# Gate units of the state space part given out row by row, convolution taps between a rope and two norms, and four smaller moves in a two-block transformer kernel

## The reference, cut to what matters

```
first_block:   xn = rmsnorm(concat(16 meta tokens, x));  proj = xn @ w_in -> q, k, v, r, a_low, u, z_gla, z_ssm
   o     = rmsnorm(gla_chunked(q, k, v, log_a)) * silu(r)      # 4 heads, key 128, value 256, chunks of 64 tokens
   y_gla = o @ w_o_gla
   y_s   = s5_ssm(u, ...)                                      # 64 groups of 16 channels, 64 complex states each
   glu   = gelu(y_s) @ w_glu + b_glu;  y_ssm = glu[:, :1024] * sigmoid(glu[:, 1024:])
   mixed = sigmoid(z_gla) * y_gla + sigmoid(z_ssm) * y_ssm
   h = h + rmsnorm(mixed @ w_out)
   h = h + rmsnorm(square(relu(rmsnorm(h) @ w_ff1)) @ w_ff2)
second_block:  z = modulated_norm(x) @ w_in_2 -> q_lat (384), kv_lat (256), k_rope (32), conv_in (1024), gates (2048)
   q, k, v from rmsnorm(q_lat) @ w_uq and rmsnorm(kv_lat) @ w_ukv, rope on 32 of 96 channels; 8 heads of attention
   u = glu_a * sigmoid(glu_b);  u = causal_depthwise_conv(u, 31 taps, 512 channels);  y_conv = silu(layernorm(u)) @ w_conv_out
   y = (g_attn * (attn @ w_o_attn) + g_conv * y_conv) @ w_out;  x = x + gate * y
   x = x + gate * hierarchical_moe(norm(x))                    # 4 groups of 8 experts, two chosen of one group
   return rmsnorm(x)
```

## Time and profile before

| what | us |
|---|---|
| median of 3 runs (lowest, highest) | 1719.71 (1713.06, 1719.83) |
| the profiled execution: its time | 1717.65 |
| the profiled execution: its span | 1715.8 |
| PE busy (matmuls) | 1647.7 |
| DVE busy | 1187.0 |
| ACT busy | 738.9 |
| POOL busy | 321.9 |

### The profile page before, as it was taken

One profiled execution on the slowest core, in us unless ns is written; L12 is line 12 of the kernel. 1 busy time (PEld: TensorE's weight loads), 2 busy tenths in 40 slices (PEclk: granted clock), 3 DMA queues, 4 the chain that ended last, 5 costly groups with the idle time before them and its releaser, 6 DMA issues.

```text
span 1715.8 us, 20745 instructions
## 1 busy us (share of the span) xinstructions
PE 1647.7 (96%) x8594; PEld 1337.3 (78%) x8594; DVE 1187.0 (69%) x1640; ACT 738.9 (43%) x1003; POOL 321.9 (19%) x193
## 2 busy tenths in 40 slices
PE   7999999999999999999999999979999998999997
PEld 7778977777888898788887899858846776777775
DVE  6998768763343359933556567986376646999998
ACT  5343555544222343222222234323476236777774
POOL 2010021214000003400000001424101004554552
PEclk9999999999999999999999999989999998999999
DMA  7345222423322243435325432211300206999994
GB/s 296 134 146 164 69 98 85 145 78 133 117 83 107 86 168 123 172 123 220 132 114 221 165 111 75 74 74 74 123 25 1 74 7 270 385 384 389 374 371 180
DMA packets 59646, 264.58 MB, mean 154 GB/s; under 512 B 21648, under 2 KB 22288, under 8 KB 33056
## 3 DMA queue, kind: packets, MB, share of 16 engines
q1 hardware_dynamic: 34896, 159.10, 25.5%
q0 software_dynamic: 15184, 99.90, 14.9%
q10 hardware_dynamic: 9472, 4.26, 0.9%
HBM read 239.80 MB, written 23.44 MB: 153 GB/s over the span
## 4 chain that ended last, share of the span: by engine, by line
PE 73%; DVE 20%; ACT 4%; issue 1%; DMA 1%; POOL 0%; SPq 0%; DVEq 0%; POOLq 0%
PE bank L389 72%; DVE bank L2547 4%; DVE wsplit L1834 2%; DVE wsplit L2818 2%; ACT wsplit L1126 1%; DVE parts L2818 1%; ACT parts L1771 1%; DVE products_early L1946 1%; DVE block_out L2860 0%; DVE weights_out_early L1968 0%; DVE products_early L1965 0%; DVE ada_sum L2399 0%; DMA cst<-in_cst 0%; PE bank L909 0%; DMA weights_out<-prep 0%
## 5 line engine op out<-in xcount | busy, mean ns | idle before, releaser
L389 PE MATMUL bank<-h_high,wsplit 128*128 128x512 f32 (+1 forms) x992 | 295.7, 379 | 14.2 <-DVE rope_tmp L2558 10.6
L1834 DVE TENSOR_TENSOR wsplit<-ring,wsplit 128x2048 fp32r<-128x2048 f32 x76 | 176.1, 2318 | 137.6 <-ACT wsplit L1126 137.6
L1126 ACT ACTIVATE wsplit<-ring 128x2048 fp32r<-128x2048 f32 x93 | 177.4, 1908 | 187.4 <-PE bank L389 180.3
L389 PEld LDWEIGHTS bank<-h_high,wsplit 128*128 128x128 f32 x992 | 182.1, 189 | 52.6 <-issue 11.3
L389 PE MATMUL bank<-xn_high,wsplit 128*128 128x512 f32 (+1 forms) x832 | 216.4, 348 | 3.4 <-DVE wsplit L1834 2.5
L389 PE MATMUL bank<-h_low,wsplit 128*128 128x512 f32 (+1 forms) x496 | 185.8, 375 | 0.0
L389 PE MATMUL bank<-f_high,wsplit 128*128 128x512 f32 (+1 forms) x576 | 173.1, 376 | 0.1
L389 PEld LDWEIGHTS bank<-xn_high,wsplit 128*128 128x128 f32 x832 | 144.7, 189 | 25.8 <-DVE wsplit L1834 2.9
L389 PE MATMUL bank<-xn_low,wsplit 128*128 128x512 f32 (+1 forms) x416 | 143.5, 345 | 0.0
L389 PEld LDWEIGHTS bank<-f_high,wsplit 128*128 128x128 f32 x576 | 105.7, 188 | 20.1 <-DVE wsplit L1834 0.3
L1834 POOL TENSOR_TENSOR wsplit<-ring,wsplit 128x2048 fp32r<-128x2048 f32 x18 | 83.3, 4625 | 197.8 <-ACT wsplit L1126 159.3
(11 more groups left out here) (534 smaller groups left out, 3411.4 us busy)
## 6 DMA issues: line engine op xcount, KB each, us to landing
ring<-in_W SPq DMA_DIRECT2D x122, 1024.0 KB, 4.8
weights_out<-prep SPq DMA_DIRECT2D x8, 864.0 KB, 5.2
prep<-weights_out_early POOLq DMA_DIRECT2D x8, 576.0 KB, 3.1
xslot<-zeros SPq DMA_DIRECT2D x7, 516.0 KB, 5.0
block<-xslot SPq DMA_DIRECT2D x6, 516.0 KB, 12.1
yslot<-block_out SPq DMA_DIRECT2D x6, 512.0 KB
prep<-turns_early POOLq DMA_DIRECT2D x8, 288.0 KB, 2.4
x_in<-in_xT SPq DMA_DIRECT2D x4, 528.0 KB, 5.3
```

The lines of the kernel that those rows point to most:

```text
L389: return g.matmul(o, l, r, start=first, stop=last_, skip_group_check=True)
L1126: g.activation(split_in(n, 0), ringt[:, n % RING, :], ACT.Copy).then_inc(*a.sig(("high", n)))
L1834: g.tensor_tensor(split_in(n, 1), ringt[:, n % RING, :], hi, SUB).then_inc(*t.sig(("low", n), ("released", n)))
```

## The change

- **Before the linear attention:** the low part of q1 moves ahead of `turns(7)`. `weights_out(7)` leaves its place ahead of `decays(1)`; `last_weights` makes the same in twelve instructions of half the size, behind the output copies of head 0, with its products in the tile `BC`.
- **Head 3 and the start of the blocks:** `head_sum(3)` goes between the two rows of unit r1; ACT's `head_root(3)` behind `spread(0)`; DVE's `head_norm(3)` behind `weights_in(1)` instead of before it.
- **Gate rows:** `one_row` gives the four rows of r2 and r3 behind blocks 1, 2, 3 and 5. ACT and POOL follow; ACT splits the unit zg0 in block 3 instead of 2.
- **Feed forward:** POOL's squares of x wait for `f_split` 15 instead of 3.
- **Convolution:** `rope` of the shared key and ten taps of group 2 before the norms, the other 21 behind them.
- **Mix:** the difference of row j is made behind product and sum of row j + 1; the low part of wo2's unit 0 behind row 4. ACT's order stays as it was.

```diff
+PLACES = (1, 2, 3, 5)
...
-            head_sum(3)
-            linear("r", 1, xr)
+            def one_row(name, j):
+                n = UNIT[name, j // 2]
+                wh, wl = weights(n, 8, 2048)
+                p.wait_ge(*at("low", n))
+                b = fresh(name, j, 0)
+                m = slice(128 * (j % 2), 128 * (j % 2) + 128)
+                for k in range(8):
+                    t = three(b, wh[:, k, m], wl[:, k, m], xr[0][1][:, k, :], xr[0][2][:, k, :], k == 0, k == 7)
+                t.then_inc(*p.sig((name, j, 0), ("used", n)))
+                banks.close(name, j, 0)
+
+            linear("r", 1, xr, after=lambda c: head_sum(3) if c == 7 else None)
...
-                if cb in (1, 4):
-                    linear("r", 2 + cb // 4, xr)
+                if cb in PLACES:
+                    one_row("r", 4 + PLACES.index(cb))
...
-            head_root(3)
             a.wait_ge(*at("end", "gla", "pe"))
             a.wait_ge(*at("end", "gla", "dve"))
             spread(0)
+            head_root(3)
...
-                if cb in (0, 2):
-                    next_high("r", 2 + cb // 2)
+                if cb in (0, 3):
+                    next_high("r", 2 + cb // 3)
...
+            def last_weights():
+                v.wait_ge(bbar_stored, 16)
+                v.wait_ge(weights_stored[1], 48)
+                for c in range(2):
...
+                    for k, (x, y, op) in enumerate(((0, 1, SUB), (1, 0, ADD))):
+                        v.wait_ge(*v.own())
+                        g.tensor_tensor(t[0], pw[x], c_r, MUL).then_inc(*v.sig())
+                        g.tensor_tensor(t[1], pw[y], c_i, MUL).then_inc(*v.sig())
+                        v.wait_ge(*v.own())
+                        g.tensor_tensor(WO[1][:, k, 288 * c:288 * c + 288], b[:, 0:288], b[:, 288:576], op).then_inc(*v.sig(("weights_out", 7)))
...
-            for cb in range(4, 8):
+            for cb in range(4, 7):
                 turns(cb)
+            next_low("q", 0)
+            turns(7)
...
-            next_low("q", 0)
             next_low("q", 1)
...
-                    weights_out(7)
...
+                if h == 0:
+                    last_weights()
...
             weights_in(0)
+            weights_in(1)
             head_norm(3)
-            weights_in(1)
...
             convolve(1)
-            convolve(2)
             v.wait_ge(*at("lat", 5, 0))
             v.wait_ge(*at("cos"))
             rope(kpe[64:96, :], banks.at("lat", 5, 0), ("free", "lat", 5, 0))
             v.end("kpe0")
+            convolve(2, 0, 10)
...
+            convolve(2, 10)
             convolve(3)
...
+            def mixed_low(j):
+                v.wait_ge(*at("m2_high", j))
+                g.tensor_tensor(m2l[:, j, :], GA[:, j, :], m2h[:, j, :].bitcast(F32), SUB).then_inc(*v.sig(("m2_split", j)))
+
+            for j in range(8):
...
+                if j:
+                    mixed_low(j - 1)
+                if j == 4:
+                    next_low("oc", 1)
+            mixed_low(7)
...
             gate_r(2)
+            gate_row(6)
             q.wait_ge(*at("gelu", 2))
             next_low("r", 3)
-            gate_r(3)
+            gate_row(7)
...
-            q.wait_ge(*at("f_split", 3))
+            q.wait_ge(*at("f_split", 15))
```

More of the change, by code:

```diff
@@ L1246, in gate_r, with gate_row @@
                 for j in (2 * i, 2 * i + 1):
-                    z = j % 2
-                    a.wait_ge(*at("r", j, 0))
-                    if j > 1:
-                        a.wait_ge(*at("r_gated", j - 2))
-                    else:
-                        a.wait_ge(*at("la_read"))
-                    b = banks.at("r", j, 0)
-                    g.activation(rt[2 * z], b, ACT.Sigmoid).then_inc(*a.sig())
-                    g.activation(rt[2 * z + 1], b, ACT.Copy).then_inc(*a.sig(("free", "r", j, 0), ("r_out", j)))
+                    gate_row(j)
+            def gate_row(j):
+                z = j % 2
+                a.wait_ge(*at("r", j, 0))
+                if j > 1:
+                    a.wait_ge(*at("r_gated", j - 2))
+                else:
+                    a.wait_ge(*at("la_read"))
+                b = banks.at("r", j, 0)
+                g.activation(rt[2 * z], b, ACT.Sigmoid).then_inc(*a.sig())
+                g.activation(rt[2 * z + 1], b, ACT.Copy).then_inc(*a.sig(("free", "r", j, 0), ("r_out", j)))
             def head_squares(h):
@@ L1706, in scalar @@
             for i in range(2):
-                next_high("oc", i)
+                if i == 0:
+                    next_high("oc", 0)
                 for j in range(4 * i, 4 * i + 4):
@@ L2531, in vector, with convolve @@
             g.tensor_copy(pos_f, pint.bitcast(I32)).then_inc(*v.sig())
-            def convolve(c):
+            def convolve(c, lo=0, hi=31):
                 cw = vec("conv_w_2").rearrange("p (c k) -> p c k", k=31)
@@ L2538, in convolve @@
                     v.wait_ge(*at("free", *lent["conv"]))
-                for k in range(31):
+                for k in range(lo, hi):
                     i = CU[:, c, k:k + 512]
@@ L2683, in vector @@
             oa_out(1)
-            for i in range(2):
-                next_low("oc", i)
-                for j in range(4 * i, 4 * i + 4):
-                    v.wait_ge(*at("oc", j, 0))
-                    v.wait_ge(*at("gc_out", j))
-                    g.tensor_tensor(GC[:, j, :], banks.at("oc", j, 0), GC[:, j, :], MUL).then_inc(*v.sig(("free", "oc", j, 0)))
-                    v.wait_ge(*v.own())
-                    g.tensor_tensor(GA[:, j, :], GA[:, j, :], GC[:, j, :], ADD).then_inc(*v.sig(("mixed2", j)))
-                    v.wait_ge(*at("m2_high", j))
-                    g.tensor_tensor(m2l[:, j, :], GA[:, j, :], m2h[:, j, :].bitcast(F32), SUB).then_inc(*v.sig(("m2_split", j)))
+            def mixed_low(j):
+                v.wait_ge(*at("m2_high", j))
+                g.tensor_tensor(m2l[:, j, :], GA[:, j, :], m2h[:, j, :].bitcast(F32), SUB).then_inc(*v.sig(("m2_split", j)))
+            for j in range(8):
+                if j == 0:
+                    next_low("oc", 0)
+                v.wait_ge(*at("oc", j, 0))
+                v.wait_ge(*at("gc_out", j))
+                g.tensor_tensor(GC[:, j, :], banks.at("oc", j, 0), GC[:, j, :], MUL).then_inc(*v.sig(("free", "oc", j, 0)))
+                v.wait_ge(*v.own())
+                g.tensor_tensor(GA[:, j, :], GA[:, j, :], GC[:, j, :], ADD).then_inc(*v.sig(("mixed2", j)))
+                if j:
[3 more added lines that the diff above has]
+            mixed_low(7)
             for i in range(4):
@@ L2923, in next_low, with gate_row @@
                     low(q, g, SPL[k])
-            def gate_r(i):
-                for j in (2 * i, 2 * i + 1):
-                    z = j % 2
-                    q.wait_ge(*at("r_out", j))
-                    q.wait_ge(*at("head", j // 2, j % 2))
-                    q.wait_ge(*q.own())
-                    g.tensor_tensor(rt[2 * z], rt[2 * z], rt[2 * z + 1], MUL).then_inc(*q.sig())
-                    q.wait_ge(*q.own())
-                    g.tensor_tensor(O[:, j, :], O[:, j, :], rt[2 * z], MUL).then_inc(*q.sig(("r_gated", j)))
+            def gate_row(j):
+                z = j % 2
+                q.wait_ge(*at("r_out", j))
+                q.wait_ge(*at("head", j // 2, j % 2))
+                q.wait_ge(*q.own())
+                g.tensor_tensor(rt[2 * z], rt[2 * z], rt[2 * z + 1], MUL).then_inc(*q.sig())
+                q.wait_ge(*q.own())
+                g.tensor_tensor(O[:, j, :], O[:, j, :], rt[2 * z], MUL).then_inc(*q.sig(("r_gated", j)))
+            def gate_r(i):
+                gate_row(2 * i)
+                gate_row(2 * i + 1)
             low_part(q, g, 0, 1)
```

11 lines of the change are left out of this document (9 added, 2 removed).

## The result

The changed kernel takes 1702.39 us (median of 6 executions, 1698.03 to 1705.39) against 1716.99 before (6 executions, 1713.06 to 1719.83): a ratio of 0.9914 with an interval of 0.9898 to 0.993. That is 14.6 us faster where 26.6 were forecast, and 0.4 us beyond the upper end of the range. The direction was right, the size was not. That 1702.39 lies near the 1702 and 1703 of the third and fourth rivals is chance: the rope's place and the mix brought at least what the forecast gave them. A second set of six executions, made later beside other kernels, gave 1703.59 and a ratio of 0.9933 (0.9919 to 0.9948).

What follows compares the result with a forecast made beforehand. PE was taken as the bound, with matmuls filling 96%, so only waits and the clock drops behind them could be won. Terms 3.9 + 4.2 + 12.6 + 5.5 + 0.4 = 26.6 off 1717.65 gave 1691 us; range 1683 to 1702.

Steps and rivals of the forecast that it cites:

- third and fourth rivals: Third: another wait takes the rope's place, 1702, chance 0.08. Fourth: row places and mix order don't help, 1703, chance 0.04.
- A: Before the linear attention: moving q1's low part forward removes PE's wait and clock drop; gain 3.9, bounds 0 and 4.4.
- What DVE does behind it up to the old place ends no later than today: Around q1's early low part: its 2.28 us only change places with `turns(7)` and `decays(0)`, which start 2.3 later.
- lie behind the output copies of head 0, where DVE waits for PE: In the linear attention: where the twelve half-size instructions, costing some 5.2 us of DVE, were said to stand.
- by my count at 2.8: At the k_in of head 1: PE's wait of 2.6 was to stay, at 2.8.
- B: Head 3 and gate rows: 14.5 us of waits and clock become 10.3; gain 4.2, bounds minus 2.4 and plus 12.2.
- I take it that the 3.9, one `toeplitz` wait and one of the two drops go: In the blocks: spread gate rows remove the 3.9 states wait, one `toeplitz` wait and a clock drop of some 2.7.
- a new wait for the states in block 7: In the blocks: named, for block 4 or 7, as a sign that the prediction is wrong; no size given.
- second rival: Blocks bound by DVE whatever PE's rows do: that part at minus 2.4, total gain 20.0, 1698; chance 0.18.
- C: The rope in the convolution: wait of 10.6 and clock of 2.0 go; gain 12.6, bounds 9 and 13.
- D: The mix: filling DVE's waits for ACT's rounding removes PE's waits and a clock drop; gain 5.5, lower bound 2.5.
- E: POOL's squares in the feed forward: 1.2 wait goes, 0.8 comes; gain 0.4, bounds minus 1.5 and plus 1.2.

Runs made afterwards that it cites:

- e2: The changed kernel with q1's low part and `weights_out(7)` back in their old places and no half-size instructions: 1700.45 us, ratio 0.9905.
- e5: The changed kernel with the edits before the linear attention and those of head 3 and the gate rows all taken back: 1698.03 us, ratio 0.9901.
- e10: The changed kernel with q1's low part and `weights_out(7)` back, `head_norm(3)` ahead of `weights_in(1)`, zg0's low part on DVE ahead of `scan(4)`: 1692.3 us.
- e11: e10 with POOL making the gate rows of r1 only behind the states of block 0: 1690.93 us, ratio 0.9852.
- e1: The changed kernel with `head_norm(3)` put back ahead of `weights_in(1)` on DVE: 1699.44 us, ratio 0.9893.
- e3: The changed kernel with `head_sum(3)`, `head_root(3)`, `head_norm(3)` and the gate units r2 and r3 as before the change: 1701.41 us, ratio 0.9909.
- e4: The changed kernel with all 31 taps of group 2 ahead of the rope again: 1715.11 us, ratio 0.999.
- e7: The changed kernel with the low part of zg0 made by DVE ahead of `scan(4)` instead of by POOL: 1696.88 us, ratio 0.9886.
- e12: The changed kernel with the mix's difference right behind each row and POOL's squares from part 3 on, as before: 1705.99 us, ratio 0.9951.
- e13: The changed kernel with q1's low part still early, but `weights_out(7)` back ahead of `decays(1)` and no half-size instructions: 1700.9 us, ratio 0.9911.
- e6: The changed kernel with `head_norm(3)` ahead of `weights_in(1)`, zg0's low part on DVE, and `weights_out(5)` and block 7's half-size instructions split around masks: 1694.78 us.

## Why the prediction was wrong

**A: forecast a gain of 3.9, found none.** The wait at q1 and the clock behind it went, as forecast. The step that failed is "What DVE does behind it up to the old place ends no later than today". The prediction has `turns(7)` and `decays(0)` start 2.3 us later and puts nothing against that, but ACT's queue hangs on `decays(0)`, and DVE's next low part on ACT's queue. In the nine profiles with the early low part, DVE's chain to the mask of head 0 starts between 126.5 and 127.9; in the five without it (before, e2, e5, e10, e11) between 124.4 and 125.4. PE then waits at the mask and passes it between 150.8 and 152.2 in the eight profiles that keep DVE's order up to it (the changed kernel twice, e1, e3, e4, e7, e12, e13), whether it lost 0 or 3.3 us of clock before. In the five without A it passes between 149.3 and 150.9 and does not wait. With the same loss of clock ahead of it, 1.7 us, e1, e3 and e7 pass at 151.0 to 151.2, e2 and e5 at 149.3 to 149.4. e6 keeps the early low part, moves three instructions behind the mask, and passes at 149.69 without a wait. The path over ACT is read from the traces; no run changes ACT's order.

The second failed step is that the twelve instructions "lie behind the output copies of head 0, where DVE waits for PE": between those copies and the idle time stands the mask of head 1, and PE waited 3.06 there. That the k_in stays waited for, "by my count at 2.8", did not come about either (and the terms given for it, 2.6 + 4 - 4.5, make 2.1). In time the kernels without A or with half of it stand at 1700.45 and 1700.9 against 1702.39 and 1703.59, with ratios whose intervals overlap, and the first column of the table spreads by as much. That A isn't worth 3.9 is shown; whether it costs 1 to 3 us or nothing in the whole time is not.

**B: forecast a gain of 4.2, found a loss.** The loss is 3.6 us in the pair of profiles, of which the clock is 3.4 (about 8.5 lost in the blocks against 5.1), and 2.8 in the stretch between e5 and e2, whose ratios to before (0.9901 and 0.9905) can't be told apart; e3 gives 1 us in time. So no gain is shown, and a loss of 0 to 3.6. The wait at `across(0)` was right to 0.4 us, with its parts (1.76 beside POOL, 3.34 for the reciprocal). Two terms failed. The clock behind it was put at 2.7 and was 5.0 (6.8 in the second profile: 5.0 in the row from 260, the rest just behind). And of "I take it that the 3.9, one `toeplitz` wait and one of the two drops go" the waits did go, but 3.43 for the states came at `across(6)`, where the `toeplitz` wait had been, with 3.4 of clock. The prediction looked for the 3.9 in block 6, and it had stood at the head of block 4. It named a new wait for the states in block 7 as a sign that it would be wrong, and that sign came. The loss is at or beyond its lower bound of minus 2.4, which its terms give if the 3.9 and the second drop stay (14.5 - 16.9), not by the words beside it. That bound is the second rival's case, but its reason (DVE is the bound whatever PE's rows do) is not the one shown. e7 removes the wait without taking work from DVE; what made it was one POOL instruction, which the change had moved from DVE's idle time onto the scan. The prediction counted POOL beside `weights_in(1)` and did not follow POOL's queue further. Behind that repair DVE may still be the bound: the 4.51 at `across(4)` in e11 speaks for it.

**C: right.** 12.6 forecast, 12.6 in the trace, 12.7 in time (e4). DVE's last tap ended at 1199.9 and PE freed POOL's copy at 1204.56: the room was there, 4.6 us.

**D: right in place.** 5.5 forecast, 6.2 in the stretch. The waits at 1356, 1367 and 1371 are gone, 1.16 + 0.90 + 1.75 = 3.8, and the drop of 1.7 behind them; 0.7 is not assigned. In e12 the waits come back without the drop, and the stretch gives 4.6.

**E: mis-sized.** 0.4 forecast, 1.8 found in the stretch. The wait of 1.2 that was to go lay where the prediction took it to lie, beside POOL's pass, and went. POOL's pass took 26.3 us (738.0 to 764.3), not 30, so the wait of 0.8 did not come. The other 0.6 is not assigned. POOL's additions took 1.28 to 1.30 us but for one of 3.23, far from the fifth rival's 3.2 for all.

**What stays open.** C, D and E make 20.6 in the stretches, and e5, which has only these, is 18.1 us faster than before in its medians (1716.09 against 1698.03). The experts' part and the clock drops of single executions lie between the two; which of them it is was not separated.

POOL beside DVE, as the traces show it: 3.30 us for an addition that needed 0.42, ending just behind POOL's instruction, and no delay for the product with a PSUM operand; e11 moves the delay with POOL. The Trainium skill (SBUF — State Buffer, "Who interferes with whom") says that a DVE instruction with two inputs in SBUF contends with a GpSimd instruction that reads SBUF, and that one with at most one such input does not, outside the modes that use two ports. The trace agrees in both.

## What to carry to other kernels

A wait that is removed is worth only what its successor on the same engine lets through: before counting it, find where the two engines meet next, at every kind of instruction (here the masks). An instruction that is moved forward delays all that it passes: follow each of those to the engine that waits for it, and back (here `decays(0)`, ACT's exponentials and split, and DVE's own next low part). When the pace of one engine changes, follow the queues of the engines that only help (here POOL): a long POOL instruction that used to lie in DVE's idle time can land on DVE's critical additions, and moving one such low part won more (6.7 us) than the whole rearrangement of the gate rows. Count a wait together with the clock drop behind it, and take both from several profiles.

## What the runs showed of the hardware

The granted clock can fall where TensorE waits for nothing, and not in every execution: 12 of the 14 profiles show 0.94 or 0.89 between 60 and 90 us, a loss of 1.8 or 3.3, though PE is busy there without a gap; two (before, and the changed kernel's second) show 1.00. The clock behind a wait varies too: 5.0 to 5.2 us were lost behind waits of 6.57 (the changed kernel) and 3.66 (e1), 6.8 behind 6.67 (the changed kernel's second profile), 3.4 behind 3.94 (before).

The time of an execution goes with its mean clock: the changed kernel's executions at 0.992 took 1698.03, those at 0.984 1706.57; the kernel before took 1713.2 to 1714.2 at 0.989 to 0.990 and 1720.25 at 0.984. At which places the slower ones lost it is not known, since only one execution of each was profiled. That spread is as large as any part of this change but C.
